# Tensor addresses, the place of lambda's series, and the engine of two low parts in a two-layer encoder kernel

## The reference

```
layer 0: x = x + mixer(rms_norm(x));   x = x + conv_ffn(rms_norm(x))
layer 1: x = x + attention(rms_norm(x)); x = x + conv_ffn(rms_norm(x)); final rms_norm

mixer(h):  a_x, a_g, b_u, b_v = split(h @ w_in)          # 4 x 512
   a_x = causal conv of width 4
   r, i = sigmoid(a_x @ w_r + b_r), sigmoid(a_x @ w_i + b_i)     # 8 heads of 64
   log_a = -8 * r * softplus(-lambda)
   y_a = scan(a = exp(log_a), u = sqrt(-expm1(2 log_a)) * i * a_x) * gelu(a_g)
   y_b = gelu(b_u) * (w_s * mask @ layer_norm(gelu(b_v)) + b_s)  # spatial, blocks of 128
   return concat(y_a, y_b) @ w_out
conv_ffn(h): g, u = split(causal conv of width 3 of h @ w_up);  (silu(g) * u) @ w_down   # 2752
```

## Time and profile before

| | |
|---|---|
| time, median of 3 runs | 1134.74 us (1133.98 to 1134.89) |
| the profiled execution's own time | 1134.91 us |
| its span, first to last instruction | 1133.1 us |
| instructions | 15509 |
| mean granted clock of TensorE | 0.992 of full speed |
| busy | PE 98%, PE's weight loads 81%, VectorE 57%, POOL 47%, ScalarE 38% |

### The profile page before, as it was taken

How to read it: one execution, slowest core, us unless ns; L and a number is a source line. 1 busy time by engine, 2 the same in 40 slices (tenths; PEclk the granted TensorE clock), 3 DMA queues, 4 the chain that set the end, 5 groups by cost and what they waited for, 6 DMA issues and landing times.

```text
span 1133.1 us, 15509 instructions
## 1 busy us (share of the span) xinstructions
PE 1112.2 (98%) x5199; PEld 918.1 (81%) x5199; DVE 650.0 (57%) x1062; ACT 435.8 (38%) x672; POOL 535.1 (47%) x417
## 2 busy tenths in 40 slices
PE   8999999999999999999999999999999999999996
PEld 6787888888888888887888888788888888888885
DVE  4776466766666632223777777666766666641103
ACT  6683433322323223323555555543223222232321
POOL 5567754444444445553332323363544444445542
PEclk9999999999999999999999999999999999999998
DMA  9263322322232233323322222132223222232302
GB/s 312 73 213 118 104 102 75 111 93 93 96 106 94 93 96 108 111 93 112 103 83 94 74 93 75 56 112 94 93 93 104 99 93 93 95 109 94 110 19 74
DMA packets 37875, 115.07 MB, mean 102 GB/s; under 512 B 4912, under 2 KB 7600, under 8 KB 37840
## 3 DMA queue, kind: packets, MB, share of 16 engines
q1 hardware_dynamic: 35520, 110.39, 29.2%
q10 hardware_dynamic: 2320, 4.21, 1.2%
HBM read 112.19 MB, written 6.59 MB: 105 GB/s over the span
## 4 chain that ended last, share of the span: by engine, by line
PE 39%; issue 32%; POOL 23%; DVE 3%; ACT 2%; DMA 0%; POOLq 0%; DVEq 0%; SPq 0%; ACTq 0%
PE bank L1218 13%; PE bank L1219 13%; PE bank L1220 13%; POOL wl L368 12%; POOL wl L367 10%; POOL mxl L392 0%; DVE x L1211 0%; ACT wh L463 0%; DMA x<-x_in 0%; ACT L496 0%; DVE bank L912 0%; DVE axc L913 0%; DVE bank L911 0%; POOLq L365 0%; ACT decay L592 0%
## 5 line engine op out<-in xcount | busy, mean ns | idle before, releaser
L367 POOL TENSOR_TENSOR wl<-raw,wh 128x512 fp32r<-128x512 f32 x190 | 249.3, 1312 | 562.0 <-ACT wh L463 561.9
L1218 PE MATMUL bank<-xh,wh 128*128 128x512 f32 x976 | 383.3, 393 | 1.9 <-DVE xl L838 1.8
L1220 PE MATMUL bank<-xh,wl 128*128 128x512 f32 x976 | 380.3, 390 | 0.0
L1219 PE MATMUL bank<-xl,wh 128*128 128x512 f32 x976 | 380.1, 389 | 0.0
L463 ACT ACTIVATE wh<-raw 128x1024 fp32r<-128x1024 f32 x190 | 201.1, 1059 | 370.8 <-PE bank L1220 326.5
L368 POOL TENSOR_TENSOR wl<-raw,wh 128x512 fp32r<-128x512 f32 x190 | 259.2, 1364 | 0.0
L1218 PEld LDWEIGHTS bank<-xh,wh 128*128 128x128 f32 x976 | 183.4, 188 | 41.9 <-DVE xl L838 2.0
L1220 PEld LDWEIGHTS bank<-xh,wl 128*128 128x128 f32 x976 | 183.3, 188 | 38.5
L1219 PEld LDWEIGHTS bank<-xl,wh 128*128 128x128 f32 x976 | 183.4, 188 | 37.1
L1218 PE MATMUL bank<-ah,wh 128*128 128x512 f32 (+1 forms) x357 | 136.3, 382 | 0.0
L1220 PE MATMUL bank<-ah,wl 128*128 128x512 f32 (+1 forms) x357 | 136.2, 381 | 0.0
(11 more groups left out here) (199 smaller groups left out, 1172.5 us busy)
## 6 DMA issues: line engine op xcount, KB each, us to landing
raw<-weights SPq DMA_DIRECT2D x190, 512.0 KB, 3.3
bias_scratch<-ext_scratch SPq DMA_DIRECT2D x1, 4096.0 KB, 19.2
bias<-bias_scratch ACTq DMA_DIRECT2D x8, 512.0 KB, 3.7
x<-x_in SPq DMA_DIRECT2D x8, 256.0 KB, 5.7
out<-x SPq DMA_DIRECT2D x4, 384.0 KB, 2.9
raw<-weights SPq DMA_DIRECT2D x4, 256.0 KB, 5.1
out<-x SPq DMA_DIRECT2D x2, 256.0 KB, 2.1
lng<-ln_g SPq DMA_DIRECT2D x1, 256.0 KB, 8.6
```

The source lines that it names most:

```text
L367: nc.gpsimd.tensor_tensor(low[:, 0:FIRST], raw[:, c % RAW, 0:FIRST], high[:, 0:FIRST], ALU.subtract)
L1218: nc.tensor.matmul(dst, w_hi_part, m_hi, start=first, stop=False)
L1219: nc.tensor.matmul(dst, w_hi_part, m_lo, start=False, stop=False)
L1220: return nc.tensor.matmul(dst, w_lo_part, m_hi, start=False, stop=last)
```

## The change

Three edits:

1. **Addresses.** par is allocated first, then a pad up to a multiple of 2048, then x, xh, xl, raw, wh, wl, rstd, acc, sq; small, bn6 and ident follow, and a second pad. So x to sq start at multiples of 2048, and so do the tensors of the stages.
2. **Lambda's series** is taken from behind the convolution to the front of VectorE's queue. Its first 12 steps stand ahead of xl[0], the other 5 between xl[0] and xl[1]; the running sum lies in PSUM bank 6 in place of SBUF. ScalarE's Exp for it and the table load for Sqrt stand ahead of the first weight half. ScalarE's wait for rate_done goes from `tanh_rate` to the front of the squares of x (bank 6 is one of theirs).
3. **v tiles 2 and 3.** Layer norm's last step leaves them in their PSUM banks (6 and 7) in place of vg, ScalarE makes the high parts from there, and VectorE the low parts, behind the first `scale_in_place`; they are gone from POOL's queue. TensorE's items 1 and 2 of the spatial mixing, which write banks 6 and 7, wait for these low parts (v_lo_dve).

```diff
+ROW = 2048
+LAM_BANK = 6
+        par = persistent("par", [P, N_PARAMS], F32)
+        persistent("pad", [P, -(-nc.sbuf_base // ROW) * ROW // 4 - nc.sbuf_base // 4], F32)
         x = persistent("x", [P, KT, T], F32)
...
-        par = persistent("par", [P, N_PARAMS], F32)
-        ident = persistent("ident", [P, P], F32)
...
         bn6 = persistent("bn6", [P, 4, 6], F32)
+        ident = persistent("ident", [P, P], F32)
+        persistent("pad2", [P, -(-nc.sbuf_base // ROW) * ROW // 4 - nc.sbuf_base // 4], F32)
...
             split_lo(14)
-            v_split_lo(2)
-            v_split_lo(3)
             split_lo(U_SGU)
...
             preload(ACT.Exp, 0)
+            act.wait_ge(lam_abs, 1)
+            nc.scalar.activation(ln_tmp, ln_var, ACT.Exp, scale=-1.0).then_inc(lam_exp, 1)
+            preload(ACT.Sqrt, 1)
             half_hi_part(0)
             act.wait_ge(gains_in, 16)
             first_hi(0)
-            act.wait_ge(lam_abs, 1)
-            nc.scalar.activation(ln_tmp, ln_var, ACT.Exp, scale=-1.0).then_inc(lam_exp, 1)
             other_half_hi(0)
-            preload(ACT.Sqrt, 1)
...
             split_hi(2)
+            act.wait_ge(rate_done, 1)
...
             sigmoids(1)
-            act.wait_ge(rate_done, 1)
             tanh_rate(0)
...
-                nc.scalar.activation(mxh[:, n], vg[:, n], ACT.Copy).then_inc(v_hi, 1)
+                nc.scalar.activation(mxh[:, n], vg[:, n] if n < 2 else bank[BV_BANKS[n]][:], ACT.Copy).then_inc(v_hi, 1)
...
+            num, den, ratio2, series = ln_tmp, ln_rstd, ln_var, bank[LAM_BANK][:, 0:4]
             dve.wait_ge(lru_in, 16)
             link(ts(lru_rate, lam, -1.0, None, ALU.mult))
             tt(ln_var, lam, lru_rate, ALU.max).then_inc(lam_abs, 1)
-            def decay_rate():
...
+            dve.wait_ge(lam_exp, 1)
+            link(ts(den, num, 2.0, None, ALU.add))
+            link(nc.vector.reciprocal(den, den))
+            link(tt(num, num, den, ALU.mult))
+            link(tt(ratio2, num, num, ALU.mult))
+            link(ts(series, ratio2, 1.0 / 17, None, ALU.mult))
+            for k in range(15, 2, -2):
+                link(stt(series, series, 1.0 / k, ratio2, ALU.add, ALU.mult))
+            norm_lo(0, 0)
+            link(stt(series, series, 1.0, num, ALU.add, ALU.mult))
+            link(ts(lru_rate, lru_rate, 0.0, None, ALU.max))
+            link(stt(lru_rate, series, 2.0, lru_rate, ALU.mult, ALU.add))
+            link(ts(lru_rate, lru_rate, -8.0, None, ALU.mult))
+            ts(lru_rate2, lru_rate, 2.0, None, ALU.mult).then_inc(rate_done, 1)
-            for m in range(KT):
+            for m in range(1, KT):
                 norm_lo(0, m)
...
             conv_taps(3)
-            decay_rate()
...
-                stt(vg[:, n], ps, ln_rstd[:, n:n + 1], lnb[:], ALU.mult, ALU.add).then_inc(ln_affine, 1)
+                stt(vg[:, n] if n < 2 else ps, ps, ln_rstd[:, n:n + 1], lnb[:], ALU.mult, ALU.add).then_inc(ln_affine, 1)
+
+            def v_split_lo(n):
+                dve.wait_ge(v_hi, n + 1)
+                tt(mxl[:, n], bank[BV_BANKS[n]][:], mxh[:, n], ALU.subtract).then_inc(v_lo_dve, 1)
...
             scale_in_place(U_BU, MIX_BANKS[0], bu_scaled)
+            v_split_lo(2)
+            v_split_lo(3)
             scale_in_place(U_BU + 1, MIX_BANKS[1], bu_scaled)
...
                     if item < 2:
-                        pe.wait_ge(v_lo, 2 * half + 2)
-                    if item < 3:
-                        pe.wait_ge(ln_affine, item + 2)
+                        pe.wait_ge(v_lo_dve if half else v_lo, 2)
+                    if item == 0:
+                        pe.wait_ge(ln_affine, 2)
+                    elif item < 3:
+                        pe.wait_ge(v_lo_dve, item)
```

More of the change, by code:

```diff
@@ L237, in trunk @@
                              "u_done", "decay_done"))
-        bv_mm, gelu_v, ln_var_done, ln_root, ln_norm, ln_affine, v_hi, v_lo = (
-            sem(n) for n in ("bv_mm", "gelu_v", "ln_var_done", "ln_root", "ln_norm", "ln_affine", "v_hi", "v_lo"))
+        bv_mm, gelu_v, ln_var_done, ln_root, ln_norm, ln_affine, v_hi, v_lo, v_lo_dve = (
+            sem(n) for n in ("bv_mm", "gelu_v", "ln_var_done", "ln_root", "ln_norm", "ln_affine", "v_hi", "v_lo", "v_lo_dve"))
         bu_scaled, ag_scaled, sgu_masked, sgu_mm, sgu_free, gelu_u, gelu_g, y_prod, y_hi, y_lo = (
```

## The result

| | before | after |
|---|---|---|
| median | 1134.82 us (1133.98 to 1135.98, 4 runs) | 1119.88 us (1119.78 to 1120.92, 4 runs) |
| profiled execution, own time / span | 1134.91 / 1133.1 us | 1119.78 / 1117.7 us |

What follows compares the result with a forecast made beforehand. TensorE was taken as the bound: matmul count times start-to-start step, plus a few stalls. Gains 10.6 + 3.95 + 0.4 + 2.8 = 17.8 us from 1134.74 gave 1117.0 us, range 1112 to 1129 (forecast case 1114 to 1119).

Steps and rivals of the forecast that it cites:

- Addresses: Matmuls moving stage tensors lose 6.7 ns a step at remainder 0, 10.6 us in all; x family (moving xh, xl) unchanged.
- Lambda's series: At the mixer's gates, moving the series early removes TensorE's 2.08 us stall and slow-clock steps: gain 3.95 us.
- If these short matmuls keep the ratio: Attention's scores and weighted values, counted as 140 units of 512 columns, gain 6.7 ns each: 0.9 us.
- the slow family: Matmuls moving stage tensors (ah, al, yh, mxh and others), at 233.4 ns a step; in the gates 24 gain 0.2 us.
- The start's 0.4 us: At the start, unit 1 begins at 14.6 us in place of 15.00: gain 0.4 us, bounds 0 and 0.65.
- The other five steps, 1.0 us: At the start, lambda's last five VectorE steps between xl[0] and xl[1] take 1.0 us; xl[1] comes about 0.65 earlier.
- 1.5 for POOL: 14.6: At the start, POOL takes 1.5 us for unit 1's first low half, so unit 1 starts at 14.6 us.
- Low parts of v: At the spatial mixing, moving v 2 and 3 from POOL to VectorE leaves a 1.2 us wait: gain 2.8 us.
- B: Rival on addresses: the 32-byte remainder isn't the cause, only 7.2 us remain, 1127.6 us; 13%.
- C: Rival on addresses: the x family gets faster too, 1058 to 1112 us; 9%.
- E: Rival on addresses: equal remainders collide and slow the x family; at 233.4 ns the time is 1137.2 us; 3%.
- D: Rival at the spatial gating: the stall of about 2 us stays whole, slow clock behind it, 1119.6 us; 12%.

Runs made afterwards that it cites:

- e4: Changed kernel with 64 bytes more behind the second pad, so the stages' tensors start at remainder 64 of 2048, x family at 0: 1122.30 us.
- e5: Changed kernel with 32 bytes more behind each of the two pads, so every tensor from x on starts at remainder 32 of 2048: 1118.87 us.
- e6: Changed kernel with wh and wl alone moved up by 32 bytes, all else at remainder 0: 1144.74 us.
- e9: Changed kernel with weights at remainder 0, xh and xl at 384, the stages' tensors at 320: 1136.92 us.
- e12: Changed kernel with weights at remainder 0, xh and xl at 192, the stages' tensors at 96: 1145.54 us.
- e1: Kernel before with the address edit alone (two pads, par and ident moved): 1126.44 us against 1135.54, ratio 0.9928.
- e3: Kernel before with the edit on v tiles 2 and 3 alone: 1131.82 us against 1135.54, ratio 0.9967.
- e2: Kernel before with the edit on lambda's series alone: 1131.40 us against 1135.54, ratio 0.9963.
- e7: Changed kernel with weights at remainder 0, xh and xl at 256, the stages' tensors at 128: 1128.19 us.
- e8: Changed kernel with VectorE's scans of tiles 2 and 3 moved behind the first scaling of a_g: 1119.36 us against 1135.05, ratio 0.9862.
- e10, e11: Not labelled in the text; apparently one of the last pair timed together: changed kernel again (1120.01 us) or its version with later scans (1118.24 us).

## Why the prediction was right, and where it was off

**Addresses.** The size and the place were right: 6.7 ns on 975 + 384 full matmuls, in four stages, and none on the x family. The reason was wrong. "I take the 6.7 ns to be the price of the 32-byte remainder" fell to e4, e5 and e6: what counts is the distance of the moving operand from the weights modulo 256, 32 before and 0 after. Both readings give the same numbers for this change, because the edit set both to 0. That was luck: with the weights moved as well (e6) ah has remainder 0 and goes at 233.3 ns. The rule of 16-byte lines in the Trainium skill's SBUF — State Buffer, section Specifications (TRN2), would have given no gain; all starts are multiples of 32, and the gain was there.

Two address terms were too large. In attention *both* operands lie in the stages' area and moved together: their distance was a multiple of 512 before, too. "If these short matmuls keep the ratio" failed there: 0.32 us in place of 0.9. That the stage's own projections (q, k, v by xh) don't gain is as forecast. And the 130 half-width matmuls, priced at half a step, went the other way. TensorE's timeline in the first half of the last tile, before and then after, 24 steps each:

```profile
1106.75 0.28 PE L1218 MATMUL bank<-ah,wh 128*128 128x256 f32 x1
...
1109.55 0.28 PE L1218 MATMUL bank<-ah,wh 128*128 128x256 f32 x1
```

```profile
1093.66 0.28 PE L1225 MATMUL bank<-al,wh 128*128 128x256 f32 x1
...
1096.54 0.28 PE L1226 MATMUL bank<-ah,wl 128*128 128x256 f32 x1
```

2.80 / 24 = 116.7 ns and 2.88 / 24 = 120.0: 3.3 ns slower at distance 0. Over both halves, in the second of which the difference is smaller, 0.3 us is lost where 0.4 was to be won, while the 455 whole matmuls of this stage gained the 3.0 forecast. The same stretch takes 117.8 ns a step at 64 and 320 (e4, e9), 118.3 at 480 (e6) and 120.0 at 96 (e12), so distance 0 isn't alone in being dear. Why a matmul of 256 columns is dearer at the distance at which one of 512 is cheaper stays open.

**Lambda's series.** Right at the gates: 4.16 us for 3.95 + 0.2 of the slow family, no new wait behind it, both margins of about 1 us held. The trace has eight slow steps behind the wait, not nine and a half; the sum went by starts and isn't touched. These steps make up some 1.6 us of the term, and they aren't certain: e1 has a wait of 2.21 us there and none of them, and whether chance or the addresses made that difference isn't shown. The start's 0.4 us wasn't there. VectorE's timeline after, at the start:

```profile
7.67 0.17 DVE L886 SCALAR_TENSOR_TENSOR bank<-bank,small 128x4 f32<-128x4 f32 x1
7.87 1.06 DVE L887 TENSOR_SCALAR small<-small 128x4 f32<-128x4 f32 x1
...
9.44 4.95 DVE L840 SCALAR_TENSOR_TENSOR xl<-x,par,xh 128x512 fp32r<-128x512 f32 x7
```

The failed step is "The other five steps, 1.0 us". One of them takes 1.06 us where 0.2 was reckoned: it starts while POOL makes a low half (7.48 to 8.90) and ends 0.02 us behind it, and in the other ten traces with lambda early it also ends 0.02 to 0.03 us behind that half. So xl[1] comes no earlier: in these eleven traces it starts at 9.01 to 9.44 us, with lambda late at 9.12 before, 9.01 (e1) and 9.51 (e3).

What unit 1 then waits for is POOL's low half, and "1.5 for POOL: 14.6" failed too. In seven traces (before, e2, e3, e4, e7, e8, e10) that half starts while VectorE still makes xl, and takes 1.41 to 1.76 us, the longer the more of VectorE's subtractions it meets: 1.73 in e2, where it was ready as early as before and unit 1 starts at 15.03. In six (after, e1, e5, e6, e11, e12) its weights land later, it starts at the end of VectorE's run or near it, and takes 1.29 to 1.32. After:

```profile
14.23 1.31 POOL L384 TENSOR_TENSOR wl<-raw,wh 128x512 fp32r<-128x512 f32 x1 [5.33 <-ACT wh L502]
```

In the fourteenth, e9, POOL comes first, VectorE's last subtraction takes 1.79 us, and TensorE waits 0.58 us for it.

Over fourteen traces unit 1 starts at 14.94 to 15.81, without order: with lambda early 14.94, 14.98, 14.99, 15.03, 15.07, 15.11, 15.13, 15.20, 15.22, 15.60 and 15.81 (e9), with lambda late 15.05 before, 15.08 (e1) and 15.44 (e3). So the gain of 0.4 is not seen, and the term is 0 within a scatter of half a microsecond. The 0.57 us lost in the trace after come from a landing: issued at 6.17 us (before at 6.22), the half landed at 13.50 where it was 12.46, behind the latest x tile of all traces (12.86, before 11.80). POOL starts 0.86 later and takes 0.32 less, which leaves 0.54. What makes a landing late was not tried.

**Low parts of v.** Right: 2.70 us for 2.8, a wait of 1.13 us from start to start for 1.2 (0.97 of it idle), no slow clock, and the exclusion of POOL's work and the scans as its cause (e8 takes it away). The Trainium skill, SBUF — State Buffer, section Who interferes with whom, says that a VectorE instruction with two SBUF inputs contends with a GpSimd one that reads SBUF; 2.2 us beside the scans against 1.28 without agree.

**The rivals.** B (1127.6 us) needs 233.4 ns after; it was 226.7. C and E need another step of the x family; it is 226.7. E's mechanism, equal remainders that collide, is the reverse of what the runs show: equal remainders are the fast case. D needs a wait of 2 us; its time, 1119.6, is nearly the one measured, but its mechanism isn't there.

## What to carry to other kernels

Where TensorE is the bound, read its step from start to start for each pair of operands, not the mean duration; when pairs of the same shape differ by 3%, compare where their tensors lie. For matmuls of 512 columns like these, lay the moving operand at a multiple of 256 bytes from the stationary one (with weight tiles 512 bytes apart, it then holds for all of them); their common remainder didn't matter (0, 32 and 128 were tried), and the pads alone were worth 0.8% here (e1). At 256 columns measure first: there it cost 3 ns a step. And when a low part or a small operation goes from GpSimd to VectorE, look at which of VectorE's two-operand instructions it pushes into GpSimd's next one: here that left 0.97 us of wait beside a gain of 2.70; moving two scans took it away and brought 0.49 us of another wait.

## What the runs showed of the hardware that had not been expected

- A 512-column matmul of this kind takes 226.7 ns from start to start if moving and stationary operand lie a multiple of 256 bytes apart, and 228.9 to 233.4 at the eight other distances measured; moving the weights alone by 32 bytes costs the whole kernel 25 us (e6 against the changed kernel's 1119.88).
- At 256 columns it isn't so: 120.0 ns at distance 0, 116.7 at 544, 117.8 at 64 and 320, 120.0 at 96.
- A wait of about 2 us isn't always followed by the slow clock: before, eight steps of 0.43 us follow 2.08 us of wait; in e1 none follows 2.21 us at the same place.
- A VectorE instruction on 128 x 4 values with a single SBUF input (TENSOR_SCALAR) takes 0.17 us alone and 1.06 us beside a GpSimd subtraction, and ends with it, while SCALAR_TENSOR_TENSOR with one operand in PSUM keeps 0.17.
- A GpSimd subtraction of 128 x 512 takes 1.29 us if it meets the last 0.13 us of VectorE's run of subtractions (e11), 1.41 if it meets 0.26 (e4), and 1.76 if it meets 0.6 (e7).
- Landings vary between executions with the same issue times: x's first tile, issued at 1.67 or 1.68 us, landed at 5.18 to 6.07 us in fourteen traces, and its eighth, issued at 5.47 or 5.48 us in twelve of them, at 11.80 to 12.45.
